# 56 low parts per layer on GpSimd, skewed top-16 searches, and picks in ten tiles each

## What is computed

```
q  = (h @ w_q).reshape(t, 8, 2, 128)
sc = einsum('thid,hikd->thik', q, keys)
top_s, top_i = top_k(sc, 16)
cand = top_s[:, :, 0, :, None] + top_s[:, :, 1, None, :]
best_s, best_pos = top_k(cand.reshape(t, 8, 256), 16)
experts = i1 * 128 + i2
gates = softmax(best_s)
act  = einsum('thkd,td->thk', u_tab[experts], h)
out  = einsum('thk,thkd->td', gates * gelu(act), v_tab[experts])
```

## Time and profile before

| | us |
|---|---|
| median of 3 runs (lowest, highest) | 3265.45 (3254.91, 3268.21) |
| the profiled execution | 3267.37 |
| its span, first to last instruction | 3265.6 |
| PE busy | 3082.0 (94%) |
| DVE busy | 2520.9 (77%) |
| ACT busy | 1511.3 (46%) |
| POOL busy | 670.1 (21%) |
| mean granted clock of PE, share of full speed | 0.973 |

### The profile page before, as it was taken

One profiled execution on the slowest core, in us unless ns is written; L12 is line 12 of the kernel. 1 busy time (PEld: TensorE's weight loads), 2 busy tenths in 40 slices (PEclk: granted clock), 3 DMA queues, 4 the chain that ended last, 5 costly groups with the idle time before them and its releaser, 6 DMA issues.

```text
span 3265.6 us, 47723 instructions
## 1 busy us (share of the span) xinstructions
PE 3082.0 (94%) x17460; PEld 2862.4 (88%) x17460; DVE 2520.9 (77%) x4372; ACT 1511.3 (46%) x2394; POOL 670.1 (21%) x575
## 2 busy tenths in 40 slices
PE   6988899999999899999989789899999998999998
PEld 3755679999999899999978468899999998999998
DVE  4564789998787688888876649999888867787887
ACT  3342224368787233333342532343878843333333
POOL 1000000033333422222200000001434343222221
PEclk8989999999999999999999899999999999999999
DMA  6524445578988999999922012365999999999996
GB/s 235 181 71 159 170 164 200 177 267 319 349 332 311 403 350 346 347 348 348 347 101 72 13 65 81 120 207 187 331 341 332 356 347 373 345 350 343 344 343 223
DMA packets 256497, 840.84 MB, mean 257 GB/s; under 512 B 23280, under 2 KB 72688, under 8 KB 248304
## 3 DMA queue, kind: packets, MB, share of 16 engines
q1 hardware_dynamic: 174000, 470.28, 40.8%
q0 software_dynamic: 80640, 318.80, 26.3%
q10 hardware_dynamic: 1728, 50.33, 3.7%
HBM read 736.56 MB, written 102.76 MB: 257 GB/s over the span
## 4 chain that ended last, share of the span: by engine, by line
PE 75%; DVE 12%; DMA 7%; ACT 4%; issue 1%; POOL 0%; DVEq 0%; SPq 0%; ACTq 0%; POOLq 0%
PE bank L784 34%; PE bank L1180 30%; PE bank L1164 5%; DMA w_raw<-wst 4%; DVE w_lo L1222 3%; PE bank L800 2%; PE bank L838 1%; ACT w_hi L540 1%; DMA activations<-act_out 1%; DMA ring<-u,gidx 1%; DMA ada_buf<-adaw 1%; DVE i L1595 1%; DVE i L1588 1%; DVE pick L1671 1%; DVE sc L1589 1%
## 5 line engine op out<-in xcount | busy, mean ns | idle before, releaser
L1222 DVE TENSOR_TENSOR w_lo<-w_raw,w_hi 128x1024 fp32r<-128x1024 f32 x596 | 730.0, 1225 | 585.7 <-ACT w_hi L540 577.3
L540 ACT ACTIVATE w_hi<-w_raw 128x1024 fp32r<-128x1024 f32 x596 | 631.6, 1060 | 1030.2 <-PE bank L784 760.2
L784 PE MATMUL bank<-hH,w_hi 128*128 128x384 f32 (+1 forms) x2656 | 948.4, 357 | 43.3 <-DVE w_lo L1222 17.8
L784 PE MATMUL bank<-hH,w_lo 128*128 128x384 f32 (+1 forms) x2656 | 927.8, 349 | 0.0
L784 PE MATMUL bank<-hL,w_hi 128*128 128x384 f32 (+1 forms) x2656 | 927.7, 349 | 0.0
L1180 PE MATMUL bank<-c_hi,w_hi 128*128 128x384 f32 x2048 | 686.2, 335 | 5.8 <-ACT act_out L716 3.2
L1180 PE MATMUL bank<-c_hi,w_lo 128*128 128x384 f32 x2048 | 684.2, 334 | 0.0
L1180 PE MATMUL bank<-c_lo,w_hi 128*128 128x384 f32 x2048 | 684.2, 334 | 0.0
L522 POOL DMA_INDIRECT ring<-u,gidx x256 | 372.9, 1457 | 1355.6 <-DVE gact L1610 763.9
L784 PEld LDWEIGHTS bank<-hH,w_hi 128*128 128x128 f32 x2656 | 504.2, 190 | 96.1 <-issue 53.9
L784 PEld LDWEIGHTS bank<-hH,w_lo 128*128 128x128 f32 x2656 | 503.0, 189 | 25.0
(11 more groups left out here) (252 smaller groups left out, 2520.0 us busy)
## 6 DMA issues: line engine op xcount, KB each, us to landing
w_raw<-wst SPq DMA_DIRECT2D x596, 512.0 KB
activations<-act_out SPq DMA_DIRECT2D x128, 384.0 KB
gate_matrices<-stage ACTq DMA_DIRECT2D x12, 4096.0 KB
act_in<-activations SPq DMA_DIRECT2D x64, 768.0 KB
gates<-gate_matrices SPq DMA_DIRECT2D x64, 768.0 KB
ada_buf<-adaw POOLq DMA_DIRECT2D x32, 1024.0 KB, 6.3
nrm<-adaw POOLq DMA_DIRECT2D x8, 1024.0 KB, 5.1
pj<-adaw POOLq DMA_DIRECT2D x4, 1024.0 KB, 5.3
```

Of the source, the lines that this page charges most:

```text
L540: nc.scalar.activation(w_hi[g % 2][:, :, :].rearrange("p a b -> p (a b)"), w_raw[:, g % RAWS, :], ACT.Copy).then_inc(s_wh, 1)
L784: last = mm(bank[s][:, 0:t.stop - t.start], a[s][:, k, :], b[:, k, t], start=(k == 0 and a is w_hi and b is hH), stop=(k == KT - 1 and a i ...
L1222: v.tensor_tensor(w_lo[g % 2][:, :, :].rearrange("p a b -> p (a b)"), w_raw[:, g % RAWS, :], w_hi[g % 2][:, :, :].rearrange("p a b -> p (a ...
```

## The change

POOL makes the low parts of 56 tiles in each layer, from query tile 2 to expert tile 41 (POOL_LO0 to POOL_LO1), with the loads of modulation chunks 11 to 23 in between in layer 0, and the first five gathers behind the low part of expert tile 20. DVE makes the others, and waits for POOL's last ahead of its own next. The searches work in skew: the first half of a row's search is mixed with the second half of the row ahead of it, values go straight to `topv`, and `sc2` gets a partner in `cand2`, as `rest`. Picks take 10 tiles each, ACT's exponential stands behind tile 4 of a pick, gathers are used from tile 40, gates are made from tile 44 to 108, and the last 20 tiles have 28 gathers. Cut to its core, `steps.mark` being a count without a wait, and with the removed `u_next(m)` shown once:

```diff
-PICK_TILES = 12
-GATE0 = 52
-GATE1 = 116
+PICK_TILES = 10
+GATE0 = 44
+GATE1 = 108
...
+POOL_LO0 = WQ0 + 2
+POOL_LO1 = U0 + NT * PICK_TILES + 2
+POOL_ADA = KT + 3
...
+PICKED = NT * PICK_TILES
...
-for _n in range(GATE0 - 4, N_KEYS):
-    U_GATHERS[_n] = 1 if len(quads_of(_n + 1)) == 2 else 2
+for _n in range(PICKED, GATE1):
+    U_GATHERS[_n] = 1 if _n < GATE0 or len(quads_of(_n + 1)) == 2 else 2
+for _n in range(GATE1, N_KEYS):
+    U_GATHERS[_n] = 2 if _n % 5 in (1, 3) else 1
+U_GATHERS[N_KEYS - 1] += UG - sum(U_GATHERS)
...
+    def mark(self, ins):
+        ins.then_inc(self.sem, 1)
+        self.n += 1
+        return self.n
...
-        v16 = sb("v16", [P, 2, NT, TOPK], where=r2)
...
-            pool.wait_ge(s_rhs, KT + 1)
-            for c in range(ADA_CHUNKS):
-                load_ada(1, c)
-            pool.wait_ge(s_adam, 2 * ADA_SETS)
+            def lo(l, n):
+                g = l * STREAM + n
+                pool.wait_ge(s_tile, g - 1)
+                pool.wait_ge(s_wh, g + 1)
+                pool.tensor_tensor(w_lo[g % 2][:, :, :].rearrange("p a b -> p (a b)"), w_raw[:, g % RAWS, :],
+                                   w_hi[g % 2][:, :, :].rearrange("p a b -> p (a b)").bitcast(F32),
+                                   ALU.subtract).then_inc(s_wl, 1)
+            def gather(l, k):
+                n = l * GATHERS + k
+                if n >= RING:
+                    pool.wait_ge(s_gd, n - RING + 1)
+                rows = u_rows[l] if k < UG else v_rows[l]
+                pool.indirect_dma_start(
+                    out=ring[:, n % RING, :], out_offset=None, in_=rows[:, :],
+                    in_offset=bass.IndirectOffsetOnAxis(ap=gidx[:, k % UG:k % UG + 1], axis=0)
+                ).then_inc(s_g[n % RING], 16)
...
-                pool.wait_ge(s_gidx, l + 1)
-                for k in range(GATHERS):
-                    n = l * GATHERS + k
-                    if n >= RING:
-                        pool.wait_ge(s_gd, n - RING + 1)
-                    rows = u_rows[l] if k < UG else v_rows[l]
-                    pool.indirect_dma_start(
-                        out=ring[:, n % RING, :], out_offset=None, in_=rows[:, :],
-                        in_offset=bass.IndirectOffsetOnAxis(ap=gidx[:, k % UG:k % UG + 1], axis=0)
-                    ).then_inc(s_g[n % RING], 16)
+                if l == 0:
+                    pool.wait_ge(s_rhs, KT + 1)
+                    for c in range(POOL_ADA):
+                        load_ada(1, c)
+                for n in range(POOL_LO0, POOL_LO1):
+                    if n == POOL_LO0:
+                        pool.wait_ge(s_wl, l * STREAM + n)
+                    lo(l, n)
+                    if l == 0 and n - POOL_LO0 + POOL_ADA < ADA_CHUNKS:
+                        load_ada(1, n - POOL_LO0 + POOL_ADA)
+                    if n == U0 + 2 * PICK_TILES:
+                        if l == 0:
+                            pool.wait_ge(s_adam, 2 * ADA_SETS)
+                        pool.wait_ge(s_gidx, l + 1)
+                        for k in range(RING):
+                            gather(l, k)
+                for k in range(RING, GATHERS):
+                    gather(l, k)
...
-                    if tt < NT and m == 6:
+                    if tt < NT and m == 4:
...
-                def best_keys(n, s):
-                    sc = lambda tt: bank[2 + s][:, tt * P:(tt + 1) * P]
-                    dve.wait_ge(s_sc, l * N_Q + n + 3)
-                    steps.settle()
-                    link(each(lambda tt: v.max(v16[:, s, tt, 0:8], sc(tt))))
-                    steps.settle()
-                    each(lambda tt: v.max_index(i16[:, s, tt, 0:8], v16[:, s, tt, 0:8], sc(tt)))
-                    ins = each(lambda tt: v.match_replace(sc2[:, tt, :], v16[:, s, tt, 0:8], sc(tt), -3.0e38))
-                    ins.then_inc(s_scv, 1)
-                    dve.wait_ge(s_scv, l * N_Q + n + 3)
-                    steps.settle()
-                    link(each(lambda tt: v.max(v16[:, s, tt, 8:16], sc2[:, tt, :])))
-                    steps.settle()
-                    link(each(lambda tt: v.max_index(i16[:, s, tt, 8:16], v16[:, s, tt, 8:16], sc2[:, tt, :])))
-                    v.tensor_copy(topv[:, :, n:n + 1, :].rearrange("p t a k -> p t (a k)"), v16[:, s, :, :])
-                    return v.tensor_copy(topi[:, :, n:n + 1, :].rearrange("p t a k -> p t (a k)"), i16[:, s, :, :])
-                lo(l, WQ0 + 2)
-                for n in range(N_Q - 1):
-                    lo(l, WQ0 + n + 3)
-                    ins = best_keys(n, n % 2)
-                link(best_keys(N_Q - 1, 1))
+                mark = steps.mark
+                scored = lambda n, tt: bank[2 + n % 2][:, tt * P:(tt + 1) * P]
+                rest = (sc2[:, :, :], cand2[:, 0:2, :].rearrange("p h (a b) -> p (h a) b", a=2))
+                def index_rows(n):
+                    return v.tensor_copy(topi[:, :, n:n + 1, :].rearrange("p t a k -> p t (a k)"), i16[:, n % 2, :, :])
+                listed = 0
+                for n in range(N_Q + 1):
+                    first = second = 0
+                    if n < N_Q:
+                        dve.wait_ge(s_sc, l * N_Q + n + 3)
+                        steps.settle()
+                        first = mark(each(lambda tt: v.max(topv[:, tt, n, 0:8], scored(n, tt))))
+                    if n >= 2:
+                        dve.wait_ge(s_dve, listed)
+                        first = mark(index_rows(n - 2))
+                    if n >= 1:
+                        dve.wait_ge(s_scv, l * N_Q + n + 2)
+                        steps.settle()
+                        second = mark(each(lambda tt: v.max(topv[:, tt, n - 1, 8:16], rest[(n - 1) % 2][:, tt, :])))
+                    if n < N_Q:
+                        dve.wait_ge(s_dve, first)
+                        steps.settle()
+                        each(lambda tt: v.max_index(i16[:, n % 2, tt, 0:8], topv[:, tt, n, 0:8], scored(n, tt)))
+                        each(lambda tt: v.match_replace(rest[n % 2][:, tt, :], topv[:, tt, n, 0:8], scored(n, tt), -3.0e38)
+                             ).then_inc(s_scv, 1)
+                    if n >= 1:
+                        dve.wait_ge(s_dve, second)
+                        steps.settle()
+                        listed = mark(each(lambda tt: v.max_index(i16[:, (n - 1) % 2, tt, 8:16], topv[:, tt, n - 1, 8:16],
+                                                                  rest[(n - 1) % 2][:, tt, :])))
+                dve.wait_ge(s_dve, listed)
+                link(index_rows(N_Q - 1))
...
-                    def u_next(m):
-                        lo(l, U0 + tt * PICK_TILES + m + 2)
...
-                    u_next(0)
...
+                dve.wait_ge(s_wl, l * STREAM + POOL_LO1)
...
```

More of the change, by code:

```diff
@@ L1646, in _ @@
                                          tv[:, :, 1, :].unsqueeze(2).broadcast_to(full), ALU.add))
-                    u_next(1)
                     link(each(lambda h: v.max(bestv[:, h, 0:8], cand[:, h, :])))
-                    u_next(2)
                     each(lambda h: v.max_index(bestp[:, h, 0:8], bestv[:, h, 0:8], cand[:, h, :]))
-                    u_next(3)
                     link(each(lambda h: v.match_replace(cand2[:, h, :], bestv[:, h, 0:8], cand[:, h, :], -3.0e38)))
-                    u_next(4)
                     link(each(lambda h: v.max(bestv[:, h, 8:16], cand2[:, h, :])))
-                    u_next(5)
                     link(each(lambda h: v.max_index(bestp[:, h, 8:16], bestv[:, h, 8:16], cand2[:, h, :])))
@@ L1661, in _ @@
                                     ALU.subtract).then_inc(s_shift, 1)
-                    u_next(6)
                     flat = bestp[:, :, :].rearrange("p h k -> p (h k)")
@@ L1672, in _ @@
                                              iota[:, 0:TOPK].unsqueeze(1).broadcast_to([P, HK, TOPK]), ALU.is_equal))
-                        u_next(7 + 2 * a)
                         link(v.tensor_tensor(pk4, pk4, ti[:, :, a, :].unsqueeze(2).broadcast_to(full), ALU.mult))
-                        u_next(8 + 2 * a)
                         if a == 0 and tt >= 2:
@@ L1690, in _ @@
                         ins.then_inc(s_rt, 1)
-                    u_next(11)
                     if tt == 0:
```

## The result

| | before | after |
|---|---|---|
| median of 10 runs each (lowest, highest), us | 3269.05 (3254.91, 3276.5) | 3282.51 (3278.33, 3290.52) |
| ratio with its 95% interval | | 1.0044 (1.0029 to 1.0060) |
| profiled execution, its span, us | 3267.37, 3265.6 | 3278.98, 3277.2 |
| mean granted TensorE clock | 0.973 | 0.973 |

The time lies in the range, but the sign is clear: some 14 us slower by the ratio, 11.6 by the profiled spans. Lines behind the change have moved: the projection of a u tile is L819 now, ACT's high part L575, Pool's low part L527, the gathers L537, and in a pick cand is L1688, the shift L1698, the equality L1709, the product L1711, the sum L1715.

A forecast was written before the change was run, and what follows sets the result against it. PE was taken to bound layer 0's query projection and the picks, DVE layer 1's query projection, with ACT, DVE and DMA near full from the first gates on. Gains of 39.5 us against losses of 39.4 gave 3265 us, range 3228 to 3312.

The forecast's parts named there:

- the query projection: Layer 1's query tiles up to expert tile 2: DVE falls below PE's 6.36 us a tile, gain 11.6 us.
- the entry in layer 0: Before expert tile 2 of layer 0: 0.88 us of waiting goes, gain 0.9 us.
- the longer first low part: Behind the pair in layer 1: Pool's first low part is some 1.1 us longer than DVE's, loss 1.1.
- the five gathers: Between low parts 20 and 21 on Pool: PE waits 5.0 us plus 1.9 for half clock, loss 13.8 in all.
- Pool's low part: Expert tiles beside the picks: 2.3 us each, fits within 2.41, costs nothing per tile.
- ACT is 1 to 1.5 late: loss 2.5 for two layers: Pick 0 of each layer: the shift is ready some 18 us after expert tile 2 starts; loss 2.5 us in all.
- A Pool operation that meets a DVE operation with two SBUF inputs waits for its end: Beside the picks: Pool's low parts wait for DVE, 2.8 us a pick, loss 22 us for eight picks.
- The third rival: Beside the picks: DVE is held by Pool as well, 36 us instead of 22, so 3279 us; chance 0.17.
- Gain 13.5 a layer, 27.0: Last 20 expert tiles of each layer: 34.3 MB at 395 GB/s take 86.8 us instead of 100.3.
- that Pool does not wait: Beside the picks: Pool's low part runs along beside DVE, 22 us less, 3243 us; chance 0.24.
- That it is longer than 2.41: Expert tiles of the picks: PE waits for Pool's low part in every tile, 3290 to 3312 us; chance 0.21.
- The tail keeps its stalls: Last expert tiles: the stalls stay because of the last gate store, 20 us more, 3285 us; chance 0.06.

The follow-up runs named there:

- e0: A kernel of its own: six of Pool's low parts in a row, alone and beside one kind of DVE or ACT work; beside DVE additions 26.2 us.

## Why the prediction was wrong

Where the working held: the query projection (11.7 for 11.6), the entry in layer 0, the longer first low part (1.17 for 1.1), the five gathers (13.1 for 13.8), Pool's low part (2.40 for 2.3), which costs nothing by itself (u10 to u20 took 41.60 in layer 0 with the PSUM operands, ten times 4.16), and the price of the holds, 17.6 for 22. Its lower bound, 3228, doesn't follow from its terms: 3243 less the 7 of a better tail is 3236.

**"ACT is 1 to 1.5 late: loss 2.5 for two layers"** is the step that failed in the picks. ACT stood 4.91 us in pick 0 of layer 0 and 6.05 in layer 1, and the late shift left 11.5 over before with the holds taken away, against 2.5. The step had the time from cand to the shift right: 18 was forecast, 18.05 and 18.04 came. Its start was wrong: cand was put level with expert tile 2, and began 2.4 us behind it in layer 0 and 5.6 in layer 1. Casts of up to 2.38 stand in the last searches; with the old order, whose casts are not held, cand came 1.6 ahead of that tile in layer 0 and 3.4 behind it in layer 1. And a stall of ACT is paid again in PE's clock: the earlier trace rows had the price of 1.9, and the step left it out.

**"A Pool operation that meets a DVE operation with two SBUF inputs waits for its end"** was half of the mechanism. The term of 22 us took DVE as never held. It is held as long as Pool is (e0: turns of 2.34 and 2.28), so an early hold makes the next one. The third rival said so and forecast 3279, the nearest to the 3282.5 of the runs, though largely by chance: it kept the 27 of the tail, and it priced the holds at 36, where they were worth 18 to 20. The Trainium skill (SBUF — State Buffer, § Who interferes with whom) states this hold, and says as well that casts and `tensor_scalar` can take part in it, that reductions don't, and that an instruction with at most one SBUF input outside the modes that use both port pairs doesn't; the probe and the versions with a PSUM operand agree on each point. The prediction took from it only the part on two inputs, and left out the casts, which the changed order put where Pool works. I gave it 0.17 because no row showed DVE waiting. But the rows of before have only gathers on Pool, and one that ran on for 0.81 inside cand left it at 2.29; no Pool instruction there reads tiles as a low part does, so that silence said nothing about one. Nor did the losses fall evenly, 2.8 for each pick: u2 to u10 took 9.4 and 11.2, u10 to u20 1.7 and 3.5, u22 to u30 nothing, u30 to u40 1.7 in both layers. In u22 to u30 only DVE's instructions were held for long (4.36); Pool's low parts there stayed at 2.88 or less, and reached 4.5 in the other stretches. The size of the two terms together, 24.5, came out at 29.1, closer than its parts deserved: one was 4.4 too high, the other 9.0 too low.

**"Gain 13.5 a layer, 27.0"**, the tail, is the step with the largest error: it gave 14.6, and with the 4.5 of the gates 19.1 (13.8 and 5.3 by layer). The forecast had 34.3 MB at 395 GB/s, 86.8 us. The last 20 tiles took 93.3 in layer 0: at 386 GB/s that is 36.0 MB, so 4.4 us went with 1.7 MB more, and 2.1 with the lower rate. In layer 1 it was 95.5, at 377 GB/s 36.0 MB as well. What the forecast put at 100.3 in the kernel before took 101.7 and 101.6. PE's wait behind a gather was indeed mostly gone, and the one behind the store of activations was not; the forecast's 86.8 left no place for it. Why the store's wait stays in every version (7.0 at most in the best one's profile) wasn't tried.

The other rivals: that Pool does not wait is excluded by 4.52 for a low part of 2.40. That it is longer than 2.41 missed by 0.01 us. "The tail keeps its stalls" was part right: it kept one of two, and its term, 20 less gain, was 12.4 in the runs.

So two terms of 24.5 and 27.0 with opposite signs were off by 4.7 and 7.9 in the same direction (12.4 for the tail itself, of which an unexplained 4.5 in the gates took some back), and nothing was left to absorb it.

## What to carry to other kernels

Work moved from DVE to Pool is paid on both: while Pool runs a tensor operation, DVE's instructions with two SBUF inputs, and its casts and scalings, take turns with it, and the durations in the profile contain the wait. Look for what DVE does beside it, and put one operand of the large ones into PSUM where a bank is free (here 0.6% of the kernel, the difference between a loss and a gain). Budget a moved step with the slack of its whole stretch: where a handoff fits by 0.01 us there is nothing to take a hold of 2 us, and a wait that stood two tiles too early in ACT's order cost some 8 us by the ratios, about what the query projection had gained alone (8.5). Read a stretch that the change only moves in more than one profile before its difference goes into a sum: the gates took 356.6 to 363.8 with the same code.

## What the runs showed of the hardware that was not expected

- Single-input DVE instructions differ: reductions and maxima run beside Pool unhindered (2278 ns against 2277; 415 against 409), casts and scalings of float32 do not (3002 against 1220). A cast of 64 columns, 0.19 alone, took up to 2.38 (2.42 with the PSUM operands).
- A two-input DVE instruction whose second operand lies in PSUM is not held, nor does it hold Pool (2.286 to 2.289 in all 32 equalities and products, Pool's low parts 2.402 in the mean and 2.47 at most), and takes no longer for it.
- Removing two stalls together gave 19 us where alone they gave 0 and 8, and with the holds gone too 46 beside the picks, where the parts gave 18.9 and 17.8: stalls that follow each other share the slack.
- A DVE instruction that comes second can lose more than one turn: an equality of 2.29 took 7.15 beside two low parts of Pool.
